# Inner feed-forward groups with the weight blocks stationary and both parts of x moving

## The reference

```python
def swiglu(h, w_gate, w_up, w_down):
    return (jax.nn.silu(h @ w_gate) * (h @ w_up)) @ w_down
...
f = swiglu(rms_norm(x, g[0]), w_ffn_gate[layer, 0], w_ffn_up[layer, 0], w_ffn_down[layer, 0])
x = x + 0.5 * rms_norm(f, g[1])
```

## Time and profile before

| | |
|---|---|
| Runs, median of 3 | 1379.26 us (1378.42 to 1379.76) |
| Profiled execution, span from first to last instruction | 1377.0 us |
| What the runs' median has above that span | 2.3 us |
| PE busy | 1359.0 us, 6525 matmuls |
| Weight loads busy | 1116.0 us |
| DVE, ACT, POOL busy | 815.2, 681.7, 41.7 us |
| Mean granted TensorE clock | 0.999 |

### The profile page before, as it was taken

How to read it: one execution, slowest core, us unless ns; L and a number is a source line. 1 busy time by engine, 2 the same in 40 slices (tenths; PEclk the granted TensorE clock), 3 DMA queues, 4 the chain that set the end, 5 groups by cost and what they waited for, 6 DMA issues and landing times.

```text
span 1377.0 us, 17411 instructions
## 1 busy us (share of the span) xinstructions
PE 1359.0 (99%) x6525; PEld 1116.0 (81%) x6525; DVE 815.2 (59%) x899; ACT 681.7 (50%) x875; POOL 41.7 (3%) x112
## 2 busy tenths in 40 slices
PE   8999999999999999999999999999999999999997
PEld 6888888888888888888887788888878778888886
DVE  5545567665555655554568855555767668654553
ACT  5444454464444554444467644444664466544442
POOL 3000000000000000000000100000000000000000
PEclk9999999999999999999999999999999999999999
DMA  8655656455556554655653265557444354565540
GB/s 294 210 192 191 222 166 217 159 165 193 185 183 215 197 183 139 192 188 183 230 182 108 93 199 193 188 183 240 163 178 153 104 175 141 191 219 190 178 166 31
DMA packets 160381, 247.09 MB, mean 179 GB/s; under 512 B 9103, under 2 KB 104649, under 8 KB 160329
## 3 DMA queue, kind: packets, MB, share of 16 engines
q1 hardware_dynamic: 160216, 246.33, 54.0%
q10 hardware_dynamic: 112, 0.05, 0.0%
HBM read 245.30 MB, written 1.05 MB: 179 GB/s over the span
## 4 chain that ended last, share of the span: by engine, by line
PE 97%; DVE 1%; ACT 1%; issue 0%; DMA 0%; POOL 0%; POOLq 0%; ACTq 0%; DVEq 0%
PE GU L575 15%; PE GU L577 15%; PE GU L576 15%; PE DD L575 12%; PE DD L577 12%; PE DD L576 12%; PE GU L640 4%; PE TB L612 3%; PE GU L647 2%; PE TB L768 2%; PE DD L1208 0%; PE GU L1473 0%; PE TB L1224 0%; PE GU L1476 0%; PE GU L1467 0%
## 5 line engine op out<-in xcount | busy, mean ns | idle before, releaser
L2155 DVE TENSOR_TENSOR wlo<-raw,whi 128x2048 fp32r<-128x2048 f32 x224 | 509.3, 2282 | 268.5 <-ACT whi L1538 268.3
L1538 ACT ACTIVATE whi<-raw 128x2048 fp32r<-128x2048 f32 x223 | 423.8, 1906 | 175.8 <-PE DD L577 167.9
L575 PE MATMUL GU<-whi,xh 128*128 128x512 f32 x928 | 367.3, 396 | 0.0
L577 PE MATMUL GU<-whi,xl 128*128 128x512 f32 x928 | 362.1, 390 | 0.0
L576 PE MATMUL GU<-wlo,xh 128*128 128x512 f32 x928 | 361.2, 389 | 0.0
L577 PEld LDWEIGHTS GU<-whi,xl 128*128 128x128 f32 x928 | 174.2, 188 | 37.3
L575 PEld LDWEIGHTS GU<-whi,xh 128*128 128x128 f32 x928 | 174.2, 188 | 35.4 <-issue 1.1
L576 PEld LDWEIGHTS GU<-wlo,xh 128*128 128x128 f32 x928 | 174.5, 188 | 34.5
L575 PE MATMUL DD<-whi,hth 128*128 128x512 f32 x496 | 194.8, 393 | 0.0
L577 PE MATMUL DD<-whi,htl 128*128 128x512 f32 x496 | 193.2, 390 | 0.0
L576 PE MATMUL DD<-wlo,hth 128*128 128x512 f32 x496 | 193.0, 389 | 0.0
(11 more groups left out here) (304 smaller groups left out, 1069.6 us busy)
## 6 DMA issues: line engine op xcount, KB each, us to landing
raw<-in_w_ffn_down SPq DMA_DIRECT2D x88, 512.0 KB, 4.2
raw<-in_w_ffn_gate SPq DMA_DIRECT2D x86, 512.0 KB, 4.0
raw<-in_w_ffn_up SPq DMA_DIRECT2D x86, 512.0 KB, 4.9
raw<-in_w_ff SPq DMA_DIRECT2D x64, 512.0 KB, 4.3
raw<-in_w_in SPq DMA_DIRECT2D x40, 512.0 KB, 4.5
raw<-in_w_conv_in SPq DMA_DIRECT2D x24, 512.0 KB, 4.8
raw<-in_w_kv SPq DMA_DIRECT2D x16, 512.0 KB, 4.8
raw<-in_w_conv_out SPq DMA_DIRECT2D x8, 512.0 KB, 4.7
```

The costliest lines, as they stand in the source:

```text
L575: pe.matmul(dst, h, w_h, start=start, stop=False)
L577: return pe.matmul(dst, l, w_h, start=False, stop=stop)
L1538: nc.scalar.activation(whi[s][:, 0:size], raw[s][:, 0:size], ACT.Copy).then_inc(hi_done[s], 1)
L2155: nc.vector.tensor_tensor(wlo[s][:, 0:size], raw[s][:, 0:size], whi[s][:, 0:size].bitcast(F32), ALU.subtract).then_inc(lo_done[s], 1)
```

## The change

In inner steps 1 to 9 (ff: 1 to 6) the first product changes sides. A block of 128x128 weights is stationary, and x moves. `xh` and `xl` lie in one tensor `xx`, so that one matmul with the high weights stationary moves both parts of all 256 rows (512 columns), and one with the low weights stationary moves `xh` alone (256 columns) into the same half of the bank. A bank (`GU` or `TB`, two banks each, the "pairs") then holds for 128 hidden columns the sum with `xh` (columns 0 to 255) and the sum with `xl` (256 to 511), and the values come out transposed. So the transposes of groups 1 to 9 (ff: 1 to 6) go. Head and tail stay as they were; the transposes of group 0 stay in step 1.

Added for it: ACT copies the second sums to `sg` (`inner_low_sums`), DVE adds the first (`inner_sums`), into `hid`. The row factors now run along the free dimension: once for each block POOL spreads them (`row_columns`), PE transposes them (`row_factors`, two blocks), ACT copies them to `rrow`, and for each group POOL multiplies both halves by them (`inner_scales`, 128x512 twice a group), before and after the gate. The two halves of e0 and the two of e1 are each taken by pairs.

```diff
+                def inner_part(e, half, pair, free=None):
+
+                    wh, wl = view(whi[e.slot], e), view(wlo[e.slot], e)
+                    for j in range(2):
+                        if free:
+                            pe.wait_ge(free[j], gu0 + 1)
+                        dst, cs = (GU, TB)[pair][:, j, :], slice((2 * pair + j) * P, (2 * pair + j + 1) * P)
+                        for k in range(4):
+                            kk = 4 * half + k
+                            pe.matmul(both(dst), wh[:, k, cs], xx[:, :, kk, :], start=(half == 0 and k == 0), stop=False)
+                            mm = pe.matmul(dst[:, 0:S], wl[:, k, cs], xh[:, kk, :], start=False, stop=(half == 1 and k == 3))
+                    return mm
...
+                def row_factors():
+
+                    pe.wait_ge(rb_ready, n.rows + 1)
+                    for t in range(TT):
+                        mm = pe.transpose(DD[:, 2, t * P:(t + 1) * P], rcols[:, t, :], ident[:, :])
+                    mm.then_inc(row_t, 1)
+                    n.rows += 1
...
-                    if g == 1:
-                        x_half(gu_banks, es[0], 0, 0, False, read=(gu_used, gu0 + 1), rows=True)
...
-                    hidden_transposes(g - 1, d)
-                    x_half(gu_banks, es[1], 1, 4, True, d=d, done=gu_ready)
...
+                def step_1(at):
+
+                    e0, e1, *ds = ent[at:at + per]
+                    pe.wait_ge(lo_done[e0.slot], e0.raw_before + 1)
+                    inner_part(e0, 0, 0, gu_used)
+                    if name == "ffn0":
+                        other_columns()
+                    row_factors()
+                    first_transposes()
+                    pe.wait_ge(lo_done[e1.slot], e1.raw_before + 1)
+                    inner_part(e1, 1, 0).then_inc(w_ready, 1)
+                    for b in range(nd):
+                        pe.wait_ge(t_used[b], t0[b] + 1)
+                    inner_part(e0, 0, 1).then_inc(used[e0.slot], 1)
+                    inner_part(e1, 1, 1).then_inc(used[e1.slot], 1)
+                    pe.wait_ge(row_ready, n.rows)
+                    if name == "ffn0":
                         pe.wait_ge(cols_ready, 2)
-                    down(g - 1, es[2:], d, start=(static and g == 1))
...
+                def step(g, at, d=0):
+
+                    e0, e1, *ds = ent[at:at + per]
+                    pe.wait_ge(w_used[0], d + w0 + g - 1)
+                    pe.wait_ge(lo_done[e0.slot], d + e0.raw_before + 1)
+                    inner_part(e0, 0, 0)
+                    pe.wait_ge(w_used[1], d + w0 + g - 1)
+                    inner_part(e0, 0, 1).then_inc(used[e0.slot], 1)
+                    pe.wait_ge(lo_done[e1.slot], d + e1.raw_before + 1)
+                    inner_part(e1, 1, 0).then_inc(w_ready, 1)
+                    inner_part(e1, 1, 1).then_inc(used[e1.slot], 1)
+                    down(g - 1, ds, d, False)
...
+                def inner_low_sums(p, g, d):
+
+                    if p == 0:
+                        act.wait_ge(w_ready, d + w0 + g)
+                    else:
+                        act.wait_ge(used[later1.slot], d + later1.split_before + g)
+                    nc.scalar.activation(both(sg[:, p, :]), pair_of(p)[:, :, 1, :], ACT.Copy).then_inc(w_copied[p], 1)
...
+                def inner_gate(g, d):
+
+                    act.wait_ge(w_scaled[0], d + w0 + g)
+                    nc.scalar.activation(sg[:, 0, :], hid[:, 0, :], ACT.Silu).then_inc(w_gate, 1)
...
-                    split(ent[e + 1])
                     split(ent[e])
                     hidden_hi(steps - 2, 0)
-                    gate_rows(steps - 1, 0, 0)
+                    split(ent[e + 1])
+                    gate_rows(1, 0)
...
+                def inner_sums(p, g, d):
+
+                    if g > 1:
+                        dve.wait_ge(w_low[p if nd == 2 else 0], d + (w0 if p == 0 or nd == 1 else 0) + g - 1)
+                    dve.wait_ge(w_copied[p], d + w0 + g)
+                    nc.vector.tensor_tensor(both(hid[:, p, :]), pair_of(p)[:, :, 0, :], both(sg[:, p, :]), ALU.add)\
+                        .then_inc(w_used[p], 1)
...
+                def inner_products(g, d):
+
+                    if nd == 1:
+                        dve.wait_ge(w_scaled[1], d + w0 + g)
+                        dve.wait_ge(w_used[1], d + w0 + g)
+                        nc.vector.tensor_tensor(hid[:, 0, :], hid[:, 1, :], sg[:, 0, :], ALU.mult).then_inc(w_hid[0], 1)
+                        return
...
+                def scale(t, made, sem, d):
+
+                    pool.wait_ge(made, d + w0 + 1)
+                    nc.gpsimd.tensor_tensor(both(t), both(t), rows2, ALU.mult).then_inc(sem, 1)
...
+                    scale(hid[:, 0, :], w_used[0], w_scaled[0], d)
+                    if nd == 1:
+                        scale(sg[:, 0, :], w_gate, w_scaled[1], d)
+                    else:
+                        scale(hid[:, 1, :], w_used[1], w_scaled[1], d)
```

More of the change, by code:

```diff
@@ L52 @@
 R_GKV, R_N1, R_N2, R_LB = 96, 104, 112, 120
+FFNS = ("ffn0", "ffn1", "ffn2", "ffn3", "ff")
 R_PEK, R_PEV, R_SUB, R_HG, N_SM2 = 24, 40, 56, 57, 58
@@ L821, in down_rows, with gate_tail @@
                     return mm
-                def gate_tail(g, e0, e1):
-                    for t in range(TT):
-                        pe.wait_ge(gu_used[t], gu0 + g)
+                def gate_tail(e0, e1):
+                    pe.wait_ge(w_used[0], w0 + steps - 2)
                     pe.wait_ge(lo_done[e0.slot], e0.raw_before + 1)
                     x_rows(gu_banks[0], e0, 0, 0)
-                    hidden_transposes(g - 1, 0)
                     pe.wait_ge(lo_done[e1.slot], e1.raw_before + 1)
@@ L1663, in step @@
                     hidden_hi(g - 1, d)
+                    if g == 1:
+                        act.wait_ge(row_t, n.rows)
+                        nc.scalar.activation(rrow, DD[:, 2, 0:S], ACT.Copy).then_inc(row_ready, 1)
                     split(ent[e + nd], d)
-                    gate(g, d)
+                    inner_low_sums(0, g, d)
+                    if nd == 1:
+                        inner_gate(g, d)
+                    inner_low_sums(1, g, d)
                     split(ent[e + nd + 1], d)
@@ L1716, in ffn @@
                     hidden_hi(steps - 2, 0)
-                    gate(steps - 1, 0)
+                    for t in range(TT):
+                        gate_rows(1, t)
                     split(ent[e + 2])
@@ L2333, in ffn @@
                     hidden_lo(steps - 2, 0)
-                    hidden(steps - 1, 0)
+                    for t in range(TT):
+                        dve.wait_ge(w_low[t], n.w if t == 0 else steps - 2)
+                        hidden_rows(1, t)
                     split(ent[e + 2])
@@ L3007, in norms, with row_columns, inner_scales, step @@
                     norm(1, ssq[:, c:c + 1], msq[:, c:c + 1], rs[:, c:c + 1], D, rs_ready)
+            done = [0]
+            def row_columns(name):
+                pool.wait_ge(rs_ready, order(name))
+                c = ncol[name]
+                nc.gpsimd.tensor_copy(rcols, rs[:, c:c + TT].unsqueeze(2).broadcast_to([P, TT, P])).then_inc(rb_ready, 1)
+            def inner_scales(name):
+                steps, nd = ffn_shape(name)
+                w0 = done[0]
+                done[0] += steps - 2
+                rows2 = rrow.unsqueeze(1).broadcast_to([P, 2, S])
+                def scale(t, made, sem, d):
+                    pool.wait_ge(made, d + w0 + 1)
+                    nc.gpsimd.tensor_tensor(both(t), both(t), rows2, ALU.mult).then_inc(sem, 1)
+                def step(d):
+                    scale(hid[:, 0, :], w_used[0], w_scaled[0], d)
+                    if nd == 1:
+                        scale(sg[:, 0, :], w_gate, w_scaled[1], d)
+                    else:
+                        scale(hid[:, 1, :], w_used[1], w_scaled[1], d)
+                row_columns({"ffn0": "pre0", "ffn1": "pre2", "ffn2": "pre4", "ffn3": "pre6", "ff": "pre8"}[name])
+                pool.wait_ge(row_ready, FFNS.index(name) + 1)
+                with pool.Fori(0, steps - 2) as i:
+                    step(i)
             chain(nc.gpsimd.memset(ident[:, :], 0.0))
@@ L3043, in _ @@
             ins.then_inc(const2, 1)
-            norms("pre0", "pre5")
+            norms("pre0", "pre0")
+            inner_scales("ffn0")
+            norms("post0", "pre2")
+            inner_scales("ffn1")
+            norms("post2", "pre3")
+            inner_scales("ffn2")
+            norms("post3", "pre5")
             pool.wait_ge(rs_ready, order("pre5"))
```

179 lines of the change are left out of this document (99 added, 80 removed).

## The result

The changed kernel takes 1385.27 us (median of 4 runs, 1384.26 to 1386.63), the kernel before 1379.46 us (4 runs, 1378.42 to 1379.76). The ratio is 1.0045, interval 1.0033 to 1.0057: slower by 0.33 to 0.57%. The profiled span goes from 1377.0 to 1382.9 us, +5.9 us, where -8.3 us was forecast. 1371.0 us was too low by 14.3, and the time lies 1.3 us above the range.

A forecast was written before the change was run, and what follows sets the result against it. PE was taken as the bound, busy 1359.0 of 1377.0 us. Terms -22.9 (transposes), +7.6 (matmuls), +1.1 (row factors) and +5.9 (waits) gave -8.3, a 1368.7 us span and 1371.0 us median; range 1360 to 1384.

The forecast's parts named there:

- Removed: PE transposes of hidden values: 36 sets of four at 0.48 us and six of eight at 0.93 go, 22.9 us less.
- The two transposes of a block's row factors: Added on PE in each block: 0.11 us per transpose, 1.1 us in ten.
- A group costs 32 x (226.7 + c) ns: Inner groups' matmuls on PE, formerly 48 x 226.7 ns: +0.18 us a group, +7.6 us over 42 groups.
- c: Distance on PE behind a 256-column matmul, taken as 119 ns, between bounds of 111 and 129.5 ns.
- rival 1: 256-column matmul not hidden over its weight load: slower, 1385 us at 129.5 ns; chance 0.13, plus 0.10 around zero.
- the sum: All terms against the profiled span: -22.9 + 7.6 + 1.1 + 5.9 = -8.3 us, from 1377.0 to 1368.7.
- The lower bound for c: 111 ns, from nine weight loads behind 30-column matmuls on PE; there the groups' term would be -3.1 us.
- Waits in step 1: PE waits for the second bank (1.17, 0.67, 0.60 us) and for TB (1.70, 1.73): 5.9 us in all.
- rival 4: Step 1's waits twice as long, a late slot delaying ACT and DVE into step 2: 1377 us; chance 0.06.
- POOL's chain: Later steps' ACT, DVE and POOL sequence, 14.1 + 2p us: costs nothing if a POOL pass p, assumed 1.5, stays under 3.9.
- the case that the prediction feared at 5.5: POOL pass slowed to 5.5 us beside DVE instructions with SBUF inputs: 134 us, about 1505 us; chance 0.04.
- The page that the prediction set aside: Trainium skill's matmul gap of N/2.4 + 2.5 ns, 109 ns for 256 columns; by it the sum is 13.4 us lower.

The follow-up runs named there:

- e0: Not a run but a name in the code: the weights of the first half of an inner step's first product, held in a slot; no measured time.
- e3: Changed kernel, but in step 1 ACT and DVE make group 0's hidden parts before splitting down's blocks, and DVE reads the second head result earlier: 1377.28 us, ratio 0.9985.
- e6: Changed kernel, but the narrow matmul moves 192 columns instead of 256: 1367.99 us.
- e9: Changed kernel, but the narrow matmul moves 224 columns instead of 256: 1373.16 us.
- e5: Changed kernel with e3's order, and from step 2 on each half issues 16 wide matmuls, then 16 narrow ones: 1369.10 us, ratio 0.9927.
- e2: Changed kernel, but both parts of x lie side by side, so a wide matmul's operand is one piece: 1384.29 us, ratio 1.0041.
- e4: Changed kernel, but the narrow matmul also moves both parts of x (512 columns), so inner groups have only wide ones: 1513.24 us.
- e10: Changed kernel, but inner groups load only 96 of the 128 columns of each weight block: 1385.46 us.
- e1: Changed kernel, but inner groups issue four wide matmuls in a row, then four narrow ones, instead of alternating: 1381.27 us, ratio 1.0011.

## Why the prediction was wrong, step by step

- **Removed: right.** The forecast had 0.48 us for four transposes and 0.93 for eight. From the start of the tail, where nothing else changes on PE, to the work behind the transposes that went, the distance between the two kernels shrinks by 0.46 to 0.49 us in the four blocks and by 0.93 in ff. The two transposes of a block's row factors have 0.108 and 0.109 us, as forecast (1.1 in all).
- **"A group costs 32 x (226.7 + c) ns": here it failed.** c = 119 was right (117 measured), and rival 1, a narrow matmul not hidden over its load, did not come. Rival 1's 1385 us is the measured time by coincidence: it had c = 129.5. But the sum took the wide matmul unchanged. It takes 236.3 ns between narrow ones, and `down` starts with ten slow distances (241, 237, 234, 235, 225, 230, 236, 229, 232, 231 ns, then 227). A step is 0.29 us above the forecast in ffn0 and in ff: 0.23 by the pairs, 0.06 by `down`. Over 42 groups that is 12.3 us, of 14.2 that the sum is off; the term is 19.9 us instead of 7.6. With it and the waits of e3 the sum is -22.9 + 19.9 + 1.1 + 7.8 = +5.9 us, the measured change of span. The lower bound for c was not one either: "faster than its load no matmul can follow", 111 ns, but single distances are 86 ns in e6 and 100 to 108 in e9, paid for by the wide one behind.
- The rows for it stood there: in the earlier trace rows the sum over 21 distances was read, and nothing behind the group; in the earlier trace rows the wide matmul behind the transposes lasts longer, which was booked as the transposes' price and not asked about behind other short matmuls. The distances of before behind the 280-column group are 235, 229, 231, 231, 236, 228, 233, 230 and then 227 ns, and e5's series is the end of this one. Behind the four transposes of the earlier trace rows they are 317 ns and then 235, 233, 236, 224, 231, 236, 228, 233, 231 before 227: of the 0.48 us, 0.05 were slow distances further on.
- **Waits in step 1: right in place and count, short in sum.** Four of five are within 0.2 us (1.19, 0.69, 0.61, 1.89 for 1.17, 0.67, 0.60, 1.73). In ffn0 it is 3.23 for 1.70: the forecast moved the times of before, and did not see that the split ahead of `hth` waits for its weights' transfer, which doesn't come earlier when the rest does. With e3 the term is 7.8 us, so 1.9 above 5.9; rival 4 had more (5.9 us on top), and its cause (a late slot into step 2) didn't show.
- **POOL's chain: right.** One pass takes 1.28 to 1.30 us in all but five cases (1.5 assumed), and PE waits nowhere for `w_used` or in `down`. The chain of one step, from the DVE sums on:

```profile
87.92 0.68 DVE L2363 TENSOR_TENSOR hid<-GU,sg 128x512 f32<-128x512 f32 x1
...
88.68 1.28 POOL L3126 TENSOR_TENSOR hid<-hid,psc 128x512 f32<-128x512 f32 x1 [13.47 <-DVE hid L2363]
89.99 0.63 ACT L1727 ACTIVATE sg<-hid 128x512 f32<-128x512 f32 x1 [2.87 <-POOL hid L3126]
...
90.70 1.30 POOL L3126 TENSOR_TENSOR sg<-sg,psc 128x512 f32<-128x512 f32 x1 [0.74 <-ACT sg L1727]
...
92.03 0.69 DVE L2371 TENSOR_TENSOR hid<-hid,sg 128x512 f32<-128x512 f32 x1
```

It began 10.07 us into the step (77.85) and ended at 14.87. The five others are in ff, where a DVE multiplication with its inputs in SBUF runs beside the first 0.52 us of the pass. They take 1.68 us, 0.4 more; this is the case that the prediction feared at 5.5:

```profile
1243.53 0.68 DVE L2375 SCALAR_TENSOR_TENSOR hid<-hid 128x512 f32<-128x512 f32 x1
1243.69 1.68 POOL L3126 TENSOR_TENSOR hid<-hid,psc 128x512 f32<-128x512 f32 x1 [0.92 <-DVE hid L2363]
```

The prediction's estimate from the Trainium skill ("GPSIMD Engine Reference", Elementwise — side-by-side cycle accounting), 1.1 us, is 0.2 low here.

- The page that the prediction set aside (the Trainium skill, "TensorE: Matmul & The Clock Gate", Back-to-back issue gap) has 109 ns for 256 columns, by a formula that it gives for an isolated matmul. The runs show 117 between wide ones and 120 in a run; no distance by that rule was seen.

What the after-effect is stays open. Shown: it is not the operand's layout (e2, e4) and not the stationary block's kind (e4); it is not the bank either, since `down`, which writes others, has it. The pair keeps its price with a shorter load (e10), though the slow distances of `down` become fewer. Fewer and longer runs of narrow ones give time back (e1, e5). But the order alone doesn't settle it. In e3, ff's step 1 has the same alternation behind its eight transposes, and there 23 pairs take 7.97 us, 347 ns each (230 and 117), that is 226.7 + 120 with nothing on top:

```profile
1204.02 0.39 PE L803 MATMUL GU<-xx,whi 128*128 128x512 f32 x1
...
1211.99 0.39 PE L589 MATMUL DD<-whi,hth 128*128 128x512 f32 x1
```

Every step behind it is back at 353 ns. So the same matmuls have two rhythms, and what goes ahead of them has a part in which one they take. No run tests what; how instructions reach PE was not looked at.

## What to carry to other kernels

When a change puts short matmuls among long ones, price the long ones behind them too: read the distances behind every existing group of short matmuls, and keep short ones in runs (of this gain of 16 us over the change, half was the order of PE's matmuls, the other half the order of a few operations in step 1's queues of ACT and DVE). When PE is made faster through a stretch, list for each wait not only the instructions ahead of the one waited for, but the transfers that these wait for: here the transfer didn't move up with PE.

## What was not expected of the hardware

- Fp32r matmuls of 512 columns, 226.7 ns apart among their like, start 224 to 241 ns apart for five to ten matmuls behind narrower ones of 128, 256 or 280 columns, and 232 to 241 apart where they alternate with 256, but 230 in ff's step 1.
- In a run, 256 columns are 120 ns apart (106.7 of streaming and 13.3). With a weight load of 128 columns before each, alternating with 512, a pair stops at 340.0 ns: 192 columns save only 3.4 ns against 224, where streaming is 13.3 shorter.
- POOL's 128x512 multiplication with both inputs in SBUF took 1.29 us, 3.4 times the 0.38 us of a 128x128 pass of another kind, and 1.68 with DVE's multiplication of 128x512 in SBUF beside it.
